# A hybrid decoder layer on one core: modulation products in groups, small inputs turned later, recurrent work spread over the parts of a step

## The chip, the cores and the metric

The kernel runs on one core of a Trainium2 chip. The metric is the device time of one execution in microseconds (us). Three runs of the kernel before gave 2319.43 to 2323.03 us, with a median of 2319.6 us.

## What is computed

One inference step of a decoder layer runs over 256 prompt columns and 8 sample columns (264 in all), with model width 2048, all in 32-bit floats:

```
mod = silu(c) @ w_ada + b_ada                     # 9 vectors sh1 sc1 g1 ... g3 of 2048, for 9 conditions
h = modulate(rmsnorm(x, g_ffn1), sh1, sc1)
x = x + 0.5 * g1 * swiglu(h, w_up1, w_down1)      # inner width 5632
h = modulate(rmsnorm(x, g_mix), sh2, sc2)
x = x + g2 * hybrid_mixer(h)                      # RG-LRU (1024 channels) and SSD (16 heads), one w_out
h = modulate(rmsnorm(x, g_ffn2), sh3, sc3)
x = x + 0.5 * g3 * swiglu(h, w_up2, w_down2)
y = modulate(rmsnorm(x, g_final), shf, scf)       # shf, scf: silu(c) @ w_ada_f, two more vectors
```

In the mixer, the RG-LRU channels pass through a causal convolution of width 4, two gates (small block-diagonal products) and a linear recurrence over time. The SSD channels pass through a convolution and a chunked scan with states. The new states are outputs too.

## The kernel before, in words

All weights stream from device memory once, 533.62 MB in the profiled execution. A weight W is split into a high part (w_hi, a rounded copy made by ScalarE, L608) and a rest (w_lo, a subtraction by VectorE, L878). TensorE makes three products of each 128 x 128 tile: w_hi with the high and with the low part of the activations, and w_lo with the high part (L1379 to L1381).

The work is a written-out list, `plan`, of **steps**. A step has four **parts** (j = 0 to 3) and each part two **pieces** of weights. The kinds of step:

- "up": 1 MB per part, 48 products of 264 columns in a part. 11 steps make a chunk; each of the two FFNs has two chunks.
- "down": three parts of 36 products and one of 24; 8 steps a chunk.
- "xbc", "dt", "lru" (4 steps), "z" (2 steps), "out" (4 steps): the mixer, in this order.

SyncE issues the loads of weights into `raw` (four buffers, one for each part) in the order of the list. The load for part j of a step waits until VectorE has split that part's pieces of the step before (`lo_done`). ScalarE and VectorE split four pieces ahead of TensorE, since w_hi and w_lo have four buffers each. All engines work their instructions off in program order.

The **modulation vectors** are made along the way. A vector takes 16 products (`ada_product`, L1343, eight instructions each, in four column tiles of the array) of 1 MB of w_ada. Vectors 0 and 1 (SH1, SC1) are made before the first step. The nine others ride on the up steps (seven vectors, four steps each) and the first four down steps of the first FFN's two chunks (two vectors): one product stands at the head of each part of such a step. Its 1 MB is loaded just behind the part's weights and waits until all but the last product before it have been made. After the fourth step ScalarE copies the sums out of PSUM (`ada_copy`, L621), TensorE turns them (`ada_turn`, L1323) and VectorE adds the bias (`mod_place`, L900). The first product of the next vector waits for that (`mod_ready`), because it uses the same PSUM bank. Where a segment of the list has two vectors, its four steps are a hardware loop of two turns (except in the first segment, which is written out).

At the start TensorE also turns the prompt and about 20 small inputs into columns (`rows_batch`): the batch for the conditions first, then one behind each of the products 2 to 11 of SH1, the small inputs last. Before those it waits for all small loads (`other_rows`, L1396), which ScalarE issues. VectorE copies each batch out (`place`), then forms the sums of squares, and then runs `mod_place(SH1)`.

In each "lru" step t, ScalarE takes two tiles of channels out of PSUM at part 1 (`conv_first`), VectorE runs the rest of the convolution of both tiles at part 1 (`conv_taps`, L1007 to L1015), and TensorE makes the gates of tile 0 after part 2 and of tile 1 after part 3 (`gates`, L1515), each after a wait for both tiles. At part 0 of the next step ScalarE makes the GELU of the gate branch and a square root (L786, L788). At part 1 of the next step, after `conv_taps`, VectorE runs the recurrence (L1165 to L1177).

Of the kernel before, what the change touches and what calls it, by code (L numbers as in the profile page):

```python
# [21 lines left out]
F32 = mybir.dt.float32  # L22
F32R = mybir.dt.float32r
# [4 lines left out]
P = 128  # L28
D = 2048
# [119 lines left out]
def build(nc, ins, outs):  # L149
    with ExitStack() as ctx:  # L150
# [16 lines left out]
        gate = sb("gate", [P, KD, 9])  # L167
# [21 lines left out]
        def layout(entries):  # L189
# [12 lines left out]
        ada, ada_sum, act_hi, act_lo = layout([  # L202
            ("ada", [P, 2, D], F32), ("ada_sum", [P, 512], F32),
            ("act_hi", [P, KC, COLS], F32R), ("act_lo", [P, KC, COLS], F32R)])

        _, _, ada_more, rowbuf, xrows = layout([
            ("ada_s", [P, 2, D], F32), ("ada_sum_s", [P, 512], F32), ("ada_more", [P, 2, D], F32),
            ("rowbuf", [P, ROW_TILES, P], F32), ("xrows", [P, 2, D], F32)])
        _, _, yrows, ysrow = layout([
            ("ada_e", [P, 2, D], F32), ("ada_sum_e", [P, 512], F32),  # L210
            ("yrows", [P, 2, D], F32), ("ysrow", [P, P], F32)])
# [37 lines left out]
        ada_landed = [sem(f"ada_landed{j}") for j in range(2)]  # L249
        first_landed = [sem(f"first_landed{j}") for j in range(4)]  # L250
# [65 lines left out]
        def ffn_plan(f, s, e, o, vec, up_vecs, down_vecs):  # L316
            for c in range(NCHUNK):
# [138 lines left out]
        def _(sp):  # L456

            def ada_load(a, vec, k):

                if not isinstance(a, int) or a >= 2:  # L460
                    sp.wait_ge(ada_used, a - 1)
# [6 lines left out]
                sp.dma_start(ada[:, k % 2, :], src).then_inc(ada_landed[k % 2], 16)  # L468

            row_copies(sp, True, c_rows)  # L470
            for a in range(2 * KD):
                if a >= 4:
                    sp.wait_ge(ada_used, a - 3)
                dst = (ada, ada_more)[(a // 2) % 2][:, a % 2, :]
                sp.dma_start(dst, w_ada[:, a % KD, bass.ds(a // KD * D, D)]).then_inc(first_landed[a % 4], 16)
# [34 lines left out]
        def _(pool):  # L510
# [8 lines left out]
            pool.memset(outcol[:, OUT_ROWS:], 0.0)  # L519
# [3 lines left out]
            pool.wait_ge(piece_used, 8 * S_XBC)  # L523
            pool.memset(spt[:, :], 0.0)  # L524
# [73 lines left out]
        def _(act):  # L598
# [113 lines left out]
            def act_tasks(kind, t, j):  # L712
# [52 lines left out]
                if kind == "lru":  # L765
# [4 lines left out]
                    if j == 3:  # L770
# [6 lines left out]
                        for h in range(2):  # L777
                            by = lam2[:, 0, 2 * t + h:2 * t + h + 1]
                            act.wait_ge(decay_ready, 2 * t + h + 1)
                            A(th[:, 0, h, :], th[:, 0, h, :], ACT.Tanh, bias=by, scale=by).then_inc(decay_tanh, 1)  # L780
                if (kind == "lru" and j == 0 and t) or (kind == "z" and u == 0):
# [5 lines left out]
                    act.wait_ge(decay_tanh, 2 * (q + 1))  # L787
                    A(th[:, 0, :, :], th[:, 0, :, :], ACT.Sqrt, scale=0.25).then_inc(sqrt_ready, 1)  # L788
# [41 lines left out]
            for n, seg in enumerate(plan):  # L830
                kind, s_first, count, per, vec0, _, _, what = seg
                nxt = last_kind(n)
                for i, last in turns(act, seg, peel_first=n == 0, peel_last=differs(n)):
                    for k in range(per):
                        s, e_, o_, par = at_step(seg, i, k)
                        follows = nxt if last and k == per - 1 else PIECE_KIND[kind]
                        for j in range(4):
                            pieces_ahead(s, j, PIECE_KIND[kind], follows)
                            if kind == "up" and j == 1:
                                act.wait_ge(piece_used, s * 8 + 4)  # L840
                                act.wait_ge(drained[1], o_)
                                A(silu_g[:, :, :], main[:, 0:2, 0:COLS], ACT.Silu).then_inc(drained[0], 1)  # L842
                            if kind not in ("up", "down"):
                                act_tasks(kind, what or 0, j)
                    if vec0 is not None:
                        ada_copy(i + vec0)
# [23 lines left out]
        def _(dve):  # L870
# [37 lines left out]
            def make_gate(vec, factor):  # L908
                dve.wait_ge(mod_ready, vec + 1)
                ch.link(TS(gate[:, :, :], mods[:, vec, :, :], factor, None, ALU.mult))  # L910
# [742 lines left out]
```

## Time and profile before

| | |
|---|---|
| median of three runs | 2319.6 us |
| the profiled execution: its own time | 2320.57 us |
| its span, first to last instruction | 2318.8 us |
| TensorE busy | 2176.4 us (94%) |
| VectorE busy | 1174.0 us (51%) |
| ScalarE busy | 843.5 us (36%) |
| GpSimd busy | 128.0 us (6%) |
| mean granted clock of TensorE | 0.968 of 2.4 GHz |
| moved by DMA | 533.62 MB, a mean of 230 GB/s |

In a timeline row the columns are: start in us, duration in us, engine, line and operation, output<-inputs, tile size, number of instructions merged, and in brackets the idle time before the row with what ended it. Durations of matmuls overlap, since they are pipelined, so the distance from start to start is what one costs. In a row of the waits the columns are: who waited, for whom, us in total, times, longest. A row of the windows gives for each engine the busy us and the count of instructions, then the granted clock, the busy share of the DMA engines and GB/s. "issue" as what ended an idle time means that the profile shows nothing the engine waited for.

### The profile page before, as it was taken

To read this page: it belongs to the slowest core of one execution; us is meant where nothing else is said; L and a number is where in the kernel's file an instruction comes from. 1 tells how busy PE (TensorE), PEld (TensorE's weight loads), DVE (VectorE), ACT (ScalarE), POOL (GpSimd) and SP (SyncE) were. 2 spreads that over 40 slices of the span, in tenths; PEclk is the share of its full clock that TensorE was granted. 3 is DMA by queue.
4 is the path that set the end of the run, shared out by engine and by line. 5 is a ranking of instruction groups with operands and counts; after the bars stand their busy time and mean duration, and the time that the engine had idled before them with its cause. 6 is when DMAs were issued, how large, how long until landed. Compare 5 with 4: busy or idle time off the path is not lost.

```text
span 2318.8 us, 41073 instructions
## 1 busy us (share of the span) xinstructions
PE 2176.4 (94%) x17101; PEld 1972.8 (85%) x17101; DVE 1174.0 (51%) x1583; ACT 843.5 (36%) x1028; POOL 128.0 (6%) x146
## 2 busy tenths in 40 slices
PE   4589999999999999989988989999999999999997
PEld 1178889889878898889987989889999988789996
DVE  1254344345433444566778876535454543344555
ACT  0143233334323333345554543433333333233333
POOL 0000000000000000001467100000000000000000
PEclk8799999999999999999998999999999999999998
DMA  8978895786878867756544555795545689795452
GB/s 345 372 248 297 279 305 192 251 301 217 303 259 290 291 204 265 265 164 184 174 149 146 158 155 178 258 310 177 181 145 177 211 284 301 257 309 181 150 185 87
DMA packets 380730, 533.62 MB, mean 230 GB/s; under 512 B 11815, under 2 KB 356783, under 8 KB 357807
## 3 DMA queue, kind: packets, MB, share of 16 engines
q1 hardware_dynamic: 358288, 519.28, 66.8%
q10 hardware_dynamic: 22303, 12.33, 1.8%
q8 instruction: 107, 1.75, 0.3%
q14 instruction: 32, 0.26, 0.0%
HBM read 524.37 MB, written 7.19 MB: 229 GB/s over the span
## 4 chain that ended last, share of the span: by engine, by line
PE 86%; DVE 7%; DMA 3%; ACT 2%; issue 1%; ACTq 1%; DVEq 0%; SPq 0%
PE main L1379 27%; PE main L1380 25%; PE main L1381 25%; PE b L1343 7%; DVE w_lo L878 2%; DMA ada_more<-in_w_ada 1%; DMA heads_row<-in_ssd_D 1%; ACT w_hi L608 0%; ACTq L445 0%; PE b L1323 0%; DVE cfull L1007 0%; DMA rowbuf<-in_b_ada 0%; DMA raw<-in_w_in 0%; DVE ntile L934 0%; DVE part L983 0%
## 5 line engine op out<-in xcount | busy, mean ns | idle before, releaser
L878 DVE TENSOR_TENSOR w_lo<-raw,w_hi 128x1024 fp32r<-128x1024 f32 (+2 forms) x720 | 797.0, 1114 | 961.6 <-ACT w_hi L608 955.6
L1379 PE MATMUL main<-h_hi,w_hi 128*128 128x264 f32 x3664 | 1069.6, 292 | 33.6 <-DVE w_lo L878 16.3
L608 ACT ACTIVATE w_hi<-raw 128x1024 fp32r<-128x1024 f32 (+2 forms) x720 | 684.0, 956 | 1119.0 <-PE main L1381 1040.9
L1380 PE MATMUL main<-h_lo,w_hi 128*128 128x264 f32 x3664 | 1052.1, 287 | 0.0
L1381 PE MATMUL main<-h_hi,w_lo 128*128 128x264 f32 x3664 | 1050.0, 287 | 0.0
L1379 PEld LDWEIGHTS main<-h_hi,w_hi 128*128 128x128 f32 x3664 | 701.6, 191 | 132.4 <-issue 111.6
L1380 PEld LDWEIGHTS main<-h_lo,w_hi 128*128 128x128 f32 x3664 | 701.1, 191 | 0.5
L1381 PEld LDWEIGHTS main<-h_hi,w_lo 128*128 128x128 f32 x3664 | 699.5, 191 | 0.0
L1379 PE MATMUL main<-act_hi,w_hi 128*128 128x264 f32 x1408 | 403.9, 287 | 0.0
L1381 PE MATMUL main<-act_hi,w_lo 128*128 128x264 f32 x1408 | 400.2, 284 | 0.0
L1380 PE MATMUL main<-act_lo,w_hi 128*128 128x264 f32 x1408 | 399.8, 284 | 0.0
L1379 PEld LDWEIGHTS main<-act_hi,w_hi 128*128 128x128 f32 x1408 | 264.7, 188 | 26.8 <-issue 18.4
L1380 PEld LDWEIGHTS main<-act_lo,w_hi 128*128 128x128 f32 x1408 | 265.4, 189 | 0.0
L1381 PEld LDWEIGHTS main<-act_hi,w_lo 128*128 128x128 f32 x1408 | 264.7, 188 | 0.0
L1343 PE MATMUL b<-ada,cT 128*32 128x512 f32 x1280 | 180.1, 628 | 33.3 <-DMA ada<-in_w_ada 12.1
L1343 PEld LDWEIGHTS b<-ada,cT 128*32 128x32 f32 x1280 | 26.1, 109 | 69.6 <-issue 25.9
L842 ACT ACTIVATE silu_g<-main 128x528 f32<-128x528 f32 x44 | 26.9, 612 | 82.5 <-PE main L1381 82.5
L524 POOL MEMSET spt<- 128x56 f32 x1 | 0.1, 144 | 1024.7 <-PE main L1381 1024.7
L1272 DVE TENSOR_TENSOR part<-silu_g,main 128x528 f32<-128x528 f32 x44 | 31.0, 704 | 32.3 <-PE main L1381 32.3
L951 DVE SCALAR_TENSOR_TENSOR x<-main,gate,x 128x256 f32<-128x256 f32 (+1 forms) x80 | 34.8, 477 | 14.2 <-PE main L1381 14.2
L621 ACT ACTIVATE ada_sum<-b 128x512 f32<-128x512 f32 x11 | 6.4, 583 | 95.0 <-PE b L1343 95.0
L1343 PE MATMUL b<-ada_more,cT 128*32 128x512 f32 x128 | 22.8, 800 | 15.0 <-DMA ada_more<-in_w_ada 15.0
(218 smaller groups left out, 765.1 us busy)
## 6 DMA issues: line engine op xcount, KB each, us to landing
raw<-in_w_up SPq DMA_DIRECT2D x176, 1024.0 KB, 7.4
ada<-in_w_ada SPq DMA_DIRECT2D x128, 1024.0 KB, 5.0
raw<-in_w_down SPq DMA_DIRECT2D x96, 768.0 KB, 4.6
raw<-in_w_in SPq DMA_DIRECT2D x36, 1024.0 KB, 5.3
ada<-in_w_ada_f SPq DMA_DIRECT2D x32, 1024.0 KB, 5.2
ada_more<-in_w_ada SPq DMA_DIRECT2D x16, 1024.0 KB, 9.1
raw<-in_w_down SPq DMA_DIRECT2D x32, 512.0 KB, 3.5
raw<-in_w_out SPq DMA_DIRECT2D x16, 1024.0 KB, 5.2
```

The costliest lines, as they stand in the source:

```text
L524: pool.memset(spt[:, :], 0.0)
L608: A(split_view(w_hi, m, kind), raw_piece(m, kind), ACT.Copy).then_inc(hi_done, 1)
L621: A(ada_sum[:, :], b4[:, :], ACT.Copy).then_inc(ada_copied, 1)
L842: A(silu_g[:, :, :], main[:, 0:2, 0:COLS], ACT.Silu).then_inc(drained[0], 1)
L878: TT(split_view(w_lo, m, kind), raw_piece(m, kind), split_view(w_hi, m, kind).bitcast(F32), ALU.subtract).then_inc(lo_done, 1)
L951: STT(xt, ps[:, h:h + 1, 0:NT], gate[:, bass.ds(n0 + h, 1), 0:1].rearrange("p a b -> p (a b)"), xt, ALU.mult, ALU.add)
L1272: TT(part[:, :, :], silu_g[:, :, :], main[:, 2:4, 0:COLS], ALU.mult).then_inc(drained[1], 1)
L1343: last = MM(b4[32 * j:32 * j + 32, :], cT[:, k, :], src[:, k % 2, j * 512:(j + 1) * 512], start=k == 0, stop=k == KD - 1, tile_position=(0 ...
L1379: MM(out, wh, hi[:, k, :], start=k == 0, stop=False)
L1380: MM(out, wh, lo[:, k, :], start=False, stop=False)
L1381: last = MM(out, wl, hi[:, k, :], start=False, stop=k == total - 1)
```

## The change

1. **Groups.** All the products of a vector for one step stand at the head of the step: four in an up step, two in a down step. The vector of a down chunk now rides on all 8 steps. `ada` has four buffers of 1 MB from the start (`ada_more` goes). Their loads are issued as one burst behind the weights of part 2 of the step before, and a load waits only for the use of its own buffer. `ada_copy`, `ada_turn` and `mod_place` move into parts 1, 2 and 3 of the vector's last step. The gates are scaled in place in `mods`; the tile `gate` and its copy for the mixer's branch go.
2. **Small inputs.** Their two batches and the spread of the heads' constants move behind products 4, 5 and 6 of SC1; VectorE runs `mod_place(SH1)` between the prompt's batches and them.
3. **Recurrent work.** The convolution of tile 0 stays at part 1 and that of tile 1 moves to part 2; gates wait for their own tile. The recurrence up to its states moves to part 0, the product with the GELU stays at part 1. The square root moves to part 3 of the step before, behind the tanh.

```diff
-        ada, ada_sum, act_hi, act_lo = layout([
-            ("ada", [P, 2, D], F32), ("ada_sum", [P, 512], F32),
...
+        ada, act_hi, act_lo = layout([
+            ("ada", [P, 4, D], F32), ("act_hi", [P, KC, COLS], F32R), ("act_lo", [P, KC, COLS], F32R)])
+        ada_sum = outcol[:, 0:512]
...
-                done = 4 * down_vecs[c]
+                done = DNS * down_vecs[c]
                 if done:
-                    plan.append(("down", s, 1, 4, vec, e, o, (f, c, 0)))
-                plan.append(("down", s + done, (DNS - done) // 2, 2, None,
-                             e + done // 2, o + done // 2, (f, c, done)))
+                    plan.append(("down", s, 1, DNS, vec, e, o, (f, c, 0)))
+                else:
+                    plan.append(("down", s, DNS // 2, 2, None, e, o, (f, c, 0)))
...
-                if not isinstance(a, int) or a >= 2:
-                    sp.wait_ge(ada_used, a - 1)
+                if not isinstance(a, int) or a >= 4:
+                    sp.wait_ge(ada_used, a - 3)
...
-                            if vec0 is not None:
+                            if vec0 is not None and j == 2:
                                 vec = i + vec0
-                                if j == 0 and k == 0 and what[0] == 1 and what[2] == 0:
+                                if k == 0 and what[0] == 1 and what[2] == 0:
                                     sp.wait_ge(h_ready, 3 * KD)
-                                ada_load(vec * KD + 4 * k + j, vec, 4 * k + j)
+                                    sp.wait_ge(stored, 16 * (len(OUT_COPIES) + 1))
+                                for q in range(k * KD // per, (k + 1) * KD // per):
+                                    ada_load(vec * KD + q, vec, q)
...
+                        act.wait_ge(decay_tanh, 2 * (t + 1))
+                        A(th[:, 0, :, :], th[:, 0, :, :], ACT.Sqrt, scale=0.25).then_inc(sqrt_ready, 1)
...
                     A(gel[:, :, :], main[:, 2:4, 0:COLS], ACT.Gelu_apprx_tanh).then_inc(drained[1], 1)
-                    act.wait_ge(decay_tanh, 2 * (q + 1))
-                    A(th[:, 0, :, :], th[:, 0, :, :], ACT.Sqrt, scale=0.25).then_inc(sqrt_ready, 1)
...
+                            if vec0 is not None and k == per - 1 and j == 1:
+                                ada_copy(i + vec0)
...
+            def conv_half(idx, j):
+
+                if j == 0:
+                    conv_free(idx)
+                marks = [None, None]
+                for w in (1, 2):
+                    conv_tile(idx, j, marks, w)
+                conv_last(idx, j, marks)
...
-                if kind == "lru" and j == 1:
-                    conv_taps(6 + t)
+                if kind == "lru" and j in (1, 2):
+                    conv_half(6 + t, j - 1)
                 if (kind == "lru" and t) or kind == "z":
                     q = t - 1 if kind == "lru" else 3
-                    if j == 1 and (kind == "lru" or t == 0):
+                    if j == 0 and (kind == "lru" or t == 0):
...
+                    if j == 1 and (kind == "lru" or t == 0):
                         dve.wait_ge(hl_ready, q + 1)
...
                             pieces_ahead(s, j, PIECE_KIND[kind], follows)
+                            if vec0 is not None and k == per - 1 and j == 3:
+                                mod_place(i + vec0)
...
-                ada_product(SH1, k, first=True)
-                if 2 <= k < 2 + batches - 1:
+                ada_product(SH1, k)
+                if 2 <= k < 2 + KD // 2:
                     rows_batch(k - 1)
...
             for k in range(KD):
-                ada_product(SC1, k, first=True)
+                ada_product(SC1, k)
+                if 4 <= k < 4 + N_ROWB:
+                    rows_batch(1 + KD // 2 + k - 4)
...
-                pe.wait_ge(conv_ready, 12 + 2 * (t // 2) + 2)
+                pe.wait_ge(conv_ready, 12 + t + 1)
...
-                            if vec0 is not None:
-                                ada_product(i + vec0, 4 * k + j)
+                            if vec0 is not None and j == 0:
+                                for q in range(k * KD // per, (k + 1) * KD // per):
+                                    ada_product(i + vec0, q)
...
+                            if vec0 is not None and k == per - 1 and j == 2:
+                                ada_turn(i + vec0)
```

`conv_tile` holds one middle tap of one tile and `conv_last` its last tap, both as they stood in `conv_taps`.

## Rows read from the trace of the kernel before

**Rows 1.** The page: busy time by engine, share of the span, instructions.
```profile
PE 2176.4 (94%) x17101; PEld 1972.8 (85%) x17101; DVE 1174.0 (51%) x1583; ACT 843.5 (36%) x1028; POOL 128.0 (6%) x146
```

**Rows 2.** Waits of TensorE: two of its nineteen groups.
```profile
PE b L1515 <- issue: 15.9, 4, 5.3
...
PE b L1343 <- DVE mods L900: 10.6, 2, 8.5
```

**Rows 3.** Timeline of TensorE: products back to back, in parts, and around plain steps.
```profile
54.91 1.07 PE L1343 MATMUL b<-ada,cT 128*32 128x512 f32 x8
55.79 1.04 PE L1343 MATMUL b<-ada_more,cT 128*32 128x512 f32 x8
...
159.82 1.07 PE L1343 MATMUL b<-ada,cT 128*32 128x512 f32 x8
...
166.83 1.06 PE L1343 MATMUL b<-ada,cT 128*32 128x512 f32 x8
...
354.25 0.60 PE L1323 MATMUL b<-ident,ada_sum 128*128 128x128 f32 x4
...
425.35 0.64 PE L1343 MATMUL b<-ada,cT 128*32 128x512 f32 x4
```

**Rows 4.** Timeline of TensorE: the start, and the first step of the second FFN.
```profile
49.70 1.08 PE L1323 MATMUL b<-ident,rowbuf 128*128 128x128 f32 x4 [8.38 <-DMA heads_row<-in_ssd_D]
...
84.36 1.94 PE L1343 MATMUL b<-ada_more,cT 128*32 128x512 f32 x8 [0.56 <-DMA ada_more<-in_w_ada]
...
104.30 1.94 PE L1343 MATMUL b<-ada_more,cT 128*32 128x512 f32 x8 [1.47 <-DMA ada_more<-in_w_ada]
...
117.58 0.59 PE L1379 MATMUL main<-h_hi,w_hi 128*128 128x264 f32 x1 [6.72 <-DVE w_lo L878]
...
138.78 1.07 PE L1343 MATMUL b<-ada,cT 128*32 128x512 f32 x8
...
1453.48 0.56 PE L1379 MATMUL main<-h_hi,w_hi 128*128 128x264 f32 x1 [4.64 <-DVE h_lo L929]
```

**Rows 5.** Timeline where one vector follows another, and branches by line.
```profile
235.31 1.23 DVE L878 TENSOR_TENSOR w_lo<-raw,w_hi 128x1024 fp32r<-128x1024 f32 x1 [2.88 <-ACT w_hi L608]
...
236.87 0.60 PE L1323 MATMUL b<-ident,ada_sum 128*128 128x128 f32 x4
...
239.55 1.02 PE L1343 MATMUL b<-ada,cT 128*32 128x512 f32 x5 [2.08 <-DVE mods L900]
...
248.15 0.64 PE L1343 MATMUL b<-ada,cT 128*32 128x512 f32 x4
...
690.20 1.05 PE L1343 MATMUL b<-ada,cT 128*32 128x512 f32 x5 [3.61 <-issue]
...
L367 PEldq COMPARE_BRANCH  x32: 76/208/4987, 376.1 to 2291.9; - x32
```

**Rows 6.** The recurrent steps: windows of two steps, and timelines of three engines.
```profile
1196.70:1238.10 41.40, 33.54 (x251) 31.12 (x250) 32.71 (x44) 20.69 (x32) 27.24 (x23) 0.92 0.50 153
1238.10:1278.00 39.90, 34.29 (x256) 33.10 (x256) 34.49 (x42) 20.85 (x30) 28.43 (x24) 0.91 0.55 166
...
1185.44 1.22 PE L1515 MATMUL b<-cval,gates_w 128*128 128x264 f32 x2 [5.00 <-issue]
...
1178.86 2.83 DVE L1007 SCALAR_TENSOR_TENSOR cfull<-cin,small,cfull 128x288 f32<-128x288 f32 x4 [0.91 <-ACT cfull L670]
...
1184.11 1.23 DVE L1015 SCALAR_TENSOR_TENSOR cval<-cin,small,cfull 128x8 f32<-128x8 f32 x1
...
1169.62 1.28 ACT L788 ACT_TABLE_LOAD   x1
```

**Rows 7.** SyncE's queue and TensorE around the last down step of a chunk; loads on the page.
```profile
564.35 0.37 SPq L489 DMA_DIRECT2D raw<-in_w_up  x1
...
573.87 0.64 PE L1343 MATMUL b<-ada,cT 128*32 128x512 f32 x4
...
ada<-in_w_ada SPq DMA_DIRECT2D x128, 1024.0 KB, 5.0
```

More of the change, by code:

```diff
@@ L248, in build @@
         w_landed = [sem(f"w_landed{j}") for j in range(4)]
-        ada_landed = [sem(f"ada_landed{j}") for j in range(2)]
-        first_landed = [sem(f"first_landed{j}") for j in range(4)]
+        ada_landed = [sem(f"ada_landed{j}") for j in range(4)]
         hi_done, lo_done = sem("hi_done"), sem("lo_done")
@@ L909, in make_gate @@
                 dve.wait_ge(mod_ready, vec + 1)
-                ch.link(TS(gate[:, :, :], mods[:, vec, :, :], factor, None, ALU.mult))
+                ch.link(TS(mods[:, vec, :, :], mods[:, vec, :, :], factor, None, ALU.mult))
             def norm_samples():
@@ L943, in norm, with add_branch @@
                 lo(KD - 1)
-            def add_branch(s, par, before, n0, squares):
+            def add_branch(vec, s, par, before, n0, squares):
                 dve.wait_ge(piece_used, s)
@@ L974, in place @@
                     dve.tensor_copy(x[:, k:k + 2, 0:NT], bank[:, :].rearrange("p (k n) -> p k n", k=2)).then_inc(rows_placed, 1)
-            for b in range(1 + N_ROWB + KD // 2):
+            for b in range(1 + KD // 2):
+                place(b)
+            mod_place(SH1)
+            for b in range(1 + KD // 2, 1 + N_ROWB + KD // 2):
                 place(b)
@@ L987, in _ @@
                     TT(sumsq[:, :, :], sumsq[:, :, :], part2[:, :, :], ALU.add).then_inc(sumsq_ready, 1)
-            mod_place(SH1)
             mod_place(SC1)
@@ L1000, in conv_taps, with conv_tile, conv_last @@
                     dve.wait_ge(gate_made, 2 * (idx - 6))
+            def conv_tile(idx, j, marks, w):
+                tap, _ = conv_params(idx, j)
+                dve.wait_ge(conv0_ready, 2 * idx + j + 1)
+                if w == 2:
+                    ch.wait(marks[j])
+                marks[j] = ch.add(STT(cfull[:, j, :], cin[:, idx % 2, j, w:w + COUT], tap(w),
+                                      cfull[:, j, :], ALU.mult, ALU.add))
+            def conv_last(idx, j, marks):
+                tap, _ = conv_params(idx, j)
+                ch.wait(marks[j])
+                STT(cval[:, j, 0:NT], cin[:, idx % 2, j, 3:3 + NT], tap(3), cfull[:, j, 0:NT], ALU.mult, ALU.add)
+                win = cfull[:, j, SAMP0 - 0:SAMP0 + 4 * NB - 3:4]
+                STT(cval[:, j, NT:COLS], windows(idx % 2)[:, j, :, 3], tap(3), win,
+                    ALU.mult, ALU.add).then_inc(conv_ready, 1)
@@ L1009, in conv_taps @@
-                        marks = [mark] if j == 0 and w == 1 else marks + [mark]
-                ch.wait()
-                for j in range(2):
-                    tap, _ = conv_params(idx, j)
-                    STT(cval[:, j, 0:NT], cin[:, r, j, 3:3 + NT], tap(3), cfull[:, j, 0:NT], ALU.mult, ALU.add)
-                    win = cfull[:, j, SAMP0 - 0:SAMP0 + 4 * NB - 3:4]
-                    STT(cval[:, j, NT:COLS], windows(r)[:, j, :, 3], tap(3), win,
-                        ALU.mult, ALU.add).then_inc(conv_ready, 1)
+                        conv_tile(idx, j, marks, w)
@@ L1280, in _ @@
                                 n0 = i * (2 * per) + 2 * (what[2] + k)
-                                add_branch(s * 8 + 8, par, (e_, o_)[par], n0, squares)
+                                add_branch((G1, G3)[what[0]], s * 8 + 8, par, (e_, o_)[par], n0, squares)
                             if kind not in ("up", "down"):
                                 dve_tasks(kind, what or 0, j, s, o_, e_)
-                    if vec0 is not None:
-                        mod_place(i + vec0)
                 if kind == "down" and squares and (n + 1 == len(plan) or plan[n + 1][0] != "down"):
@@ L1327, in turn_part, with ada_product @@
                 return MM(out, src, ident[0:rows, 0:rows], start=True, stop=True)
-            def ada_product(vec, k, first=False):
-                if first:
-                    src = (ada, ada_more)[(k // 2) % 2]
-                    pe.wait_ge(first_landed[k % 4], 16 * (vec * 4 + k // 4 + 1))
-                else:
-                    src = ada
-                    pe.wait_ge(ada_landed[k % 2], (vec - 2) * (8 * 16) + 16 * (k // 2 + 1))
+            def ada_product(vec, k):
+                pe.wait_ge(ada_landed[k % 4], vec * (4 * 16) + 16 * (k // 4 + 1))
                 if k == 0:
```

54 lines of the change are left out of this document (20 added, 34 removed).

## The prediction

> **What bounds the kernel now.** I read the page first. TensorE is busy 94% of the span, and the other engines half of it or less [rows 1], so a gain is either TensorE work that gets cheaper or a gap of TensorE that closes. The waits of TensorE, read next, show which gaps lie near the change: four waits of the gates (15.9 us, put down to "issue", though a row below shows whom they wait for) and two waits of products for `mods` (10.6 us, of which 8.5 at the start) [rows 2]. Then I went through TensorE's timeline stage by stage. In the steps that carry a vector TensorE has no gap at all: a product costs it array time and nothing else. At the start it waits for loads. In the recurrent steps it waits for VectorE. The change touches all three.
>
> **1. Products in groups.** Three plain up steps run from the turn at 354.25 to the product at 425.35: 71.1 us less about 0.5 for the turn is 23.5 us a step, 5.88 a part. A part with a product takes 166.83 - 159.82 = 7.01 us, so a product between pieces costs 1.13 us. Two products back to back start 55.79 - 54.91 = 0.88 us apart [rows 3]. Each product that joins another saves therefore 0.25 us, and a little more for those inside a run; I take 0.26. Bounds: 0, if the one back-to-back pair is a lucky case, and 0.30.
> Of 28 up steps with a vector, the first of each FFN belongs to other terms. The other 26 merge three times: 26 x 3 x 0.26 = 20.3 us. The two down vectors have 32 products in 16 groups: 16 x 0.26 = 4.2 us. Spreading them over 8 steps instead of 4 changes nothing else for TensorE. Together 24.5 us (0 to 28).
> In the second FFN's first step TensorE is idle 4.64 us before its first piece, waiting for the norm [rows 4]. All four products now stand in or ahead of that gap, three more than before: 3 x 1.13 = 3.4 us (2 to 6; at the top the clock, which stands at half after this gap, does not fall).
>
> **2. Where one vector follows another.** Before, the sums are turned at 236.87, and the next product starts at 239.55 after 2.08 us of waiting for `mod_place`; the next part begins at 248.15 [rows 5]. That is 11.3 us for a turn (0.4) and a part (7.01), so 3.9 us are lost, a part of it to the half clock that follows the wait. After the change the turn stands at part 2 and `mod_place` in VectorE's part 3, just behind a split that ended at 235.31 + 1.23 = 236.54 [rows 5]. With about 0.5 us of its own it ends some 0.2 us after TensorE gets there. I leave 0.4 and take 3.5 us (2 to 4).
> The other two places (turn at 686 and 1973) are back edges of hardware loops. There the product came after 3.61 us of "issue", and the branch in TensorE's queue takes up to 4.99 us against a median of 0.21 [rows 5]. The change keeps these loops with bodies as long as before, so the branch stays. I take 0.7 us each, 1.4 in all (0 to 16: the top is both stalls hidden).
>
> **3. The start.** TensorE sits idle for 8.38 us before 49.70, until the last small load has landed, with eleven products made; `mods` cost 8.5 more [rows 2, 4]. With at most four loads outstanding the loads run dry in both. Undisturbed they come (104.30 - 84.36) / 8 = 2.49 us apart [rows 4]. From 41.3 us, 21 products at that pace need 52.3, and the last ends near 95 instead of 106.2. The small loads now have until product 20 (near 65 us) and share the DMA engines longer, which I charge 1 us.
> Not all of these 11 us arrive. The first step now wants four products at its head, and their loads come behind 3 MB of weights: 7 MB at 2.49 us or somewhat more land at about 112, so the first piece starts near 113 instead of 117.58. Its eight pieces need 23.5 us and, by my estimate, 1.5 for the norm, which feeds the first four pieces only as it goes. The second step starts near 138. Before, it started at 138.78 + 7.01 = 145.8 [rows 4]. Gain 8 us (5 to 11).
>
> **4. Recurrent steps.** The four middle taps of both tiles run from 1178.86, the last taps end at 1184.11 + 1.23 = 1185.34, and the gates start at 1185.44 after 5.00 us: this "issue" wait is for VectorE's convolution [rows 6]. One tile is half of it, about 3.3 us instead of 6.5. The first gates start some 3 us earlier, the second tile runs while TensorE works on the next pieces, and the recurrence moves into a gap that VectorE has in part 0. With less idle time the half clock of this stretch goes in part.
> What limits the gain is VectorE: it is busy 32.71 of 41.40 us in one step and 34.49 of 39.90 in the next [rows 6], so a step cannot lose more than about 7 us. I take 4 us for three steps, 12 in all. Bounds: 4 (1.3 a step, if the moved square root delays the splits as much as the halves hasten the gates) and 20.
> The square root costs a table load of 1.28 us [rows 6]. Before, it stood beside the GELU's load. Now one more set of functions comes between exponentials, so up to one load is added per step, and the first splits of the next step stand 1.9 us later (load and root) with about 1 us of slack: that is in the 4 us. The Trainium skill ("ScalarE: Activation LUTs", section "Table sets: the hidden batching unit") prices a change of set at about 2.7 us, and says that tanh and square root are in different sets. By that the delay grows by 1.4 us in three steps and the forecast by up to 4; the trace has 1.28 for it, and the sum goes by the trace.
>
> **5. What the burst costs.** Before, each 1 MB of `w_ada` came behind 1 MB of weights. Now four stand behind the weights of part 2, and the weights of part 3 behind them. In a steady step those weights are let go when piece 5 is split, about 12.5 us into a step of 27. A load alone lands in 5.0 us [rows 7] and each further one 2.49 later, so the fourth product's lands at about 12.5 + 5.0 + 4 x 2.49 = 27.5 us and is used at 27.2 + 2.6 = 29.8. That holds by some 2 us.
> It does not hold where an up step with a vector follows a down step, which is shorter. There the weights go at 564.35 and the products start at 573.87 [rows 7]. The fourth load lands near 564.7 + 5.0 + 10 = 579.7, its product wants it at 576.5. This happens twice: I charge 3 us each, 6 in all (0 to 12).
> The gates scaled in place and the copy that goes are VectorE work of a fraction of a microsecond behind TensorE's pieces: nothing.
>
> **Sum.** 24.5 + 3.4 + 3.5 + 1.4 + 8 + 12 = 52.8, less 6 and 0.4 for small waits: 46.4 us. The profiled execution's own time is 2320.57, its span 2318.8, so 2274; the median of the runs is 1 us lower. Two of my terms (the merge inside a run and the late burst) are on the careful side, and I say **2272 us**.
>
> **The rivals.**
> *The burst comes late in every step* (slower). Margin 2 us. If VectorE splits piece 5 later than I think, or the loads run slower in a burst, each of 26 steps waits for its fourth product. A wait of 2.08 us was followed by a part of 8.60 instead of 7.01 us [rows 5], so a wait of 1 us may cost 2.6 with the half clock: 26 x 2.6 = 68, 2340 us. It decides from 1.8 us a step on, that is, from loads some 3 us later than computed. Against it: the same bytes flow now without a gap. 5%.
> *VectorE binds the recurrent steps*: the wait moves from the gates to the splits, and only some 3 of the 12 us are left: 2281. For it: GpSimd is busy 27 us of each such step [rows 6], and does the same work in a shorter step. The Trainium skill ("SBUF — State Buffer", section "SBUF: two separate sides") says that the port these two engines share is an exclusive lock, held for a whole instruction. By that VectorE's busy time would not shrink with the step, and its 33 to 34 us are the floor; I counted with it. 15%.
> *A product in a group costs what it costs alone*: 24.5 us go, 2296. Against it stands the pair in [rows 3]. 6%.
> *The loops' back edges are hidden too*, since the turn no longer stands before the branch: 13 us more, 2259. Against it: the branch reaches only some 2 us ahead of the array, and takes 5. 9%.
> *The parts eat each other up* and nothing measurable is left: 2%.
>
> **How the numbers follow.** The forecast has 63%; its terms, each to its bounds but not all at once, spread it over some 2258 to 2286. The range reaches to the VectorE and the back-edge rival and leaves out the slower one and half of the one on groups: 2252 to 2290. A difference of 0.2% is about what a measurement of this kernel can tell from no change. Faster 93%, same 2%, slower 5%.
>
> **What would show it.** Steady up steps with a vector 27.2 to 27.3 us apart, the four products within 3.5 us and without a gap; 2.0 us for two in a down step; no wait of 8 us before 60 us, and the last product of SC1 near 95; a gap under 1 us between the second and third vector, but 5-us branches still there in the two loops; gates of tile 0 waiting under 2 us, recurrent steps of 36 to 38 us; a wait of some 3 us for loads at the first products after each down chunk. Wrong would make it above all a wait for w_ada at every group, or a clock at half in the steps with products.

## The result, and the profile after

The changed kernel takes **2268.5 us** (median of four runs, 2266.8 to 2269.1) against 2320.0 us of the kernel before, measured beside it. The ratio is 0.9779, with a 95% interval from 0.9764 to 0.9793. Its profiled execution has a span of 2266.4 us, 52.4 less than before. The forecast was 2272 us, in a range of 2252 to 2290.

The head of the page shows what kind of gain it is. TensorE's busy time fell by 33.6 us [rows 1] and its share rose to 95%; so part of the gain is cheaper products, and the rest are gaps.

```profile
PE 2142.8 (95%) x17101; PEld 1968.3 (87%) x17101; DVE 1173.7 (52%) x1582; ACT 848.9 (37%) x1031; POOL 126.5 (6%) x146
```

The waits of TensorE over the whole span (who, for whom, total, times, longest) answer to [rows 2]:

```profile
PE b L1356 <- DMA ada<-in_w_ada: 45.4, 42, 7.2
PE b L1356 <- issue: 9.1, 2, 4.6
...
PE b L1529 <- DVE cval L1013: 5.6, 2, 2.8
...
PE b L1356 <- DMA ada<-in_w_ada_f: 2.9, 2, 1.5
PE b L1529 <- issue: 2.4, 2, 1.7
```

L1356 is the product (L1343 before) and L1529 the gates (L1515 before). The four waits of the gates went from 15.9 us to 8.0 (5.6 + 2.4). Most of the 45.4 us for w_ada lies at the start; from 143 us on there are 6.6 of them, and 2.9 for the last two vectors' loads, where the kernel before had none. The two waits put down to "issue" are the back edges of the two loops.

TensorE's timeline, place by place:

```profile
138.76 2.78 PE L1356 MATMUL b<-ada,cT 128*32 128x512 f32 x24
141.87 1.06 PE L1356 MATMUL b<-ada,cT 128*32 128x512 f32 x8 [0.33 <-DMA ada<-in_w_ada]
...
166.53 3.64 PE L1356 MATMUL b<-ada,cT 128*32 128x512 f32 x32
...
193.76 3.64 PE L1356 MATMUL b<-ada,cT 128*32 128x512 f32 x32
...
549.86 1.92 PE L1356 MATMUL b<-ada,cT 128*32 128x512 f32 x16 [1.50 <-DVE mods L895]
552.34 1.06 PE L1356 MATMUL b<-ada,cT 128*32 128x512 f32 x8 [0.55 <-DMA ada<-in_w_ada]
554.91 1.06 PE L1356 MATMUL b<-ada,cT 128*32 128x512 f32 x8 [1.50 <-DMA ada<-in_w_ada]
...
666.33 5.15 PE L1356 MATMUL b<-ada,cT 128*32 128x512 f32 x32 [4.57 <-issue]
...
1402.69 3.64 PE L1356 MATMUL b<-ada,cT 128*32 128x512 f32 x32
...
1433.74 1.92 PE L1356 MATMUL b<-ada,cT 128*32 128x512 f32 x16
1436.72 1.06 PE L1356 MATMUL b<-ada,cT 128*32 128x512 f32 x8 [1.06 <-DMA ada<-in_w_ada]
...
1929.94 6.51 PE L1356 MATMUL b<-ada,cT 128*32 128x512 f32 x32 [4.56 <-issue]
```

The steady step is 193.76 - 166.53 = 27.23 us long, against 4 x 7.01 = 28.04 before [rows 3], with its four products in one run of 3.64 us. The second step starts at 138.76. At 549.86, behind the first down chunk, the group takes 6.11 us instead of 3.64, because its last two products wait for their loads. At 666.33, behind a loop's back edge, it takes 5.15 without any wait for a load: the granted clock of that stretch is 0.70, that is, partly at 1.2 GHz, after 4.57 us of idling. At 1929.94, behind the other loop's back edge, it takes 6.51 at 0.55.

The gain of each stage, from start to start in the two timelines, beside the terms of the prediction:

| term | predicted | measured |
|---|---|---|
| products in groups, 26 up steps | 20.3 | 21 (26 x 0.81) |
| the same, two down vectors | 4.2 | 2.5, with 3.1 lost in groups that late loads made longer |
| first step of the second FFN | 3.4 | 4.3 |
| second vector to third | 3.5 | 3.6 |
| two back edges | 1.4 | 3.3 (2.8 and 0.5) |
| start | 8 | 14.0 |
| recurrent steps | 12 | 8.2 |
| late bursts in up steps, by the length of the groups | -6 | -8.9 (2.5, 2.9, 3.5) |
| other waits | -0.4 | -1.5 (for `mods`, at 549.86) |
| not foreseen: xbc stage, output stage | 0 | 5.1 (3.0 and 2.1) |
| sum | 46.4 | 51.6 of 52.4 |

### The profile page after: what moved, and what is told of

The parts are those of the page before. It is cut to its first block, busy times and chain, and to the rows that moved or that the text cites. A ratio compares the mean times of both kernels' runs of the same rounds, so it can differ in the third digit from the quotient of the medians.

```text
span 2266.4 us, 40943 instructions
## 1 busy us (share of the span) xinstructions
PE 2142.8 (95%) x17101; PEld 1968.3 (87%) x17101; DVE 1173.7 (52%) x1582; ACT 848.9 (37%) x1031; POOL 126.5 (6%) x146
## 4 chain that ended last, share of the span: by engine, by line
PE 80%; DMA 8%; DVE 7%; ACT 2%; issue 1%; POOL 1%; SPq 1%; ACTq 0%; DVEq 0%; POOLq 0%
PE main L1392 25%; PE main L1393 24%; PE main L1394 24%; DMA ada<-in_w_ada 7%; PE b L1356 6%; DVE w_lo L873 2%; ACT w_hi L603 1%; DMA ada<-in_w_ada_f 1%; DVE ntile L929 1%; DVE h_lo L924 0%; SPq L464 0%; PE b L1341 0%; DVE rec L1187 0%; POOL state L566 0%; DVE rstd L917 0%
## 5 line engine op out<-in xcount | busy, mean ns | idle before, releaser
L1392 PE MATMUL main<-h_hi,w_hi 128*128 128x264 f32 x3664 | 1056.2, 288 | 19.3 <-DVE h_lo L924 7.9
L1356 PE MATMUL b<-ada,cT 128*32 128x512 f32 x1408 | 189.7, 658 | 59.7 <-DMA ada<-in_w_ada 45.4
L1356 PEld LDWEIGHTS b<-ada,cT 128*32 128x32 f32 x1408 | 38.4, 114 | 164.9 <-DMA ada<-in_w_ada 92.4
L946 DVE SCALAR_TENSOR_TENSOR x<-main,mods,x 128x256 f32<-128x256 f32 (+1 forms) x80 | 34.8, 476 | 12.9 <-PE main L1394 12.9
L616 ACT ACTIVATE outcol<-b 128x512 f32<-128x512 f32 x11 | 6.5, 592 | 83.0 <-PE b L1356 83.0
L1297 DVE TENSOR_TENSOR act_lo<-part,act_hi 128x528 f32 (+1 forms) x44 | 31.2, 708 | 4.0
```

The lines of the kernel that those rows point to most:

```text
L616: A(ada_sum[:, :], b4[:, :], ACT.Copy).then_inc(ada_copied, 1)
L946: STT(xt, ps[:, h:h + 1, 0:NT], mods[:, vec, bass.ds(n0 + h, 1), 0:1].rearrange("p a b -> p (a b)"), xt, ALU.mult, ALU.add)
L1297: TT(act_lo[:, bass.ds(pair * 2, 2), :], part[:, :, :], hi.bitcast(F32), ALU.subtract).then_inc(act_ready, 1)
L1356: last = MM(b4[32 * j:32 * j + 32, :], cT[:, k, :], ada[:, k % 4, j * 512:(j + 1) * 512], start=k == 0, stop=k == KD - 1, tile_position=(0 ...
L1392: MM(out, wh, hi[:, k, :], start=k == 0, stop=False)
```

## The experiments

Each run is an edit of the changed kernel (2268.5 us, span 2266.4), and was timed against the kernel before. A time is the median of its runs; "span" is how much longer the span of its one profiled execution is than 2266.4 us.

**Products taken apart.** One product per part again, loads, copy, turn and bias as they stood before.

```diff
-                            if vec0 is not None and j == 0:
-                                for q in range(k * KD // per, (k + 1) * KD // per):
-                                    ada_product(i + vec0, q)
+                            if vec0 is not None and (per == 4 or j % 2 == 0):
+                                ada_product(i + vec0, 4 * k + j if per == 4 else 2 * k + j // 2)
...
```

> The changed kernel (2268.5 us) with its products taken apart again: one product at the head of each part of an up step, one at parts 0 and 2 of a down step, each load behind that part's weights, the sums copied and turned behind the last step; four buffers, the small inputs and the recurrent steps stay as changed. Theory (a product in a group is 0.27 us cheaper, and the boundary between vectors is hidden): a steady up step goes back from 27.22 to 28.05 us, the boundary between the second and third vector gets its 2 us wait back, the late bursts (some 13 us of waits for loads) go; in sum 25 us slower, 2290 to 2297. Rival (most of the gain came from the loads and buffers, a product costs the same alone): steps stay near 27.3 us and the time rises by 3 to 8 us, 2272 to 2276.

2294.0 us, ratio 0.9888 (0.9868 to 0.9909), span +24.4. The step is back at four parts of 7.02 us, and so is the wait at the boundary:

```profile
204.57 1.07 PE L1356 MATMUL b<-ada,cT 128*32 128x512 f32 x8
211.59 1.06 PE L1356 MATMUL b<-ada,cT 128*32 128x512 f32 x8
...
228.20 1.06 PE L1356 MATMUL b<-ada,cT 128*32 128x512 f32 x8 [2.08 <-DVE mods L895]
```

The theory holds: groups and boundaries, less the late bursts that came with them, are nearly half of the gain of 51.5 us.

**Small inputs back in the first vector.** The batches and the heads' constants go back behind products 10 to 12 of SH1.

```diff
-            for b in range(1 + KD // 2):
-                place(b)
-            mod_place(SH1)
-            for b in range(1 + KD // 2, 1 + N_ROWB + KD // 2):
+            for b in range(1 + N_ROWB + KD // 2):
                 place(b)
...
+            mod_place(SH1)
             mod_place(SC1)
...
```

> The changed kernel with the batches of small inputs and of the heads' constants back behind the products 10 to 12 of the first vector, and its bias added only after the sums of squares. Theory (the whole gain of the start is the move of the small inputs): the wait of some 8 us before 60 us comes back, the last product of SC1 ends near 106 us instead of 94.2, and the time is 10 to 14 us longer, 2278 to 2283. Rival (the start gains because four buffers and four products at the head of the first step let the loads run on): the last product of SC1 moves, but the first step's end stays within 3 us of 138.8, 2269 to 2272.

2283.7 us, ratio 0.9838 (0.9822 to 0.9854), span +15.2, just over the top of the theory. Both stops are back (L1339 is the turn, L1354 the product in this kernel):

```profile
50.04 1.08 PE L1339 MATMUL b<-ident,rowbuf 128*128 128x128 f32 x4 [10.42 <-DMA heads_row<-in_ssd_D]
...
68.68 3.64 PE L1354 MATMUL b<-ada,cT 128*32 128x512 f32 x16 [8.31 <-DVE mods L895]
```

The second step starts at 149.3 instead of 138.8.

**The recurrent part, in pieces.** Three things changed there: the halves (the convolution of the two tiles at two parts), the early recurrence and the early root. Four runs take back all of it, the root alone, the root and the early recurrence (so that only the halves stay), and the halves alone.

```diff
-                        act.wait_ge(decay_tanh, 2 * (t + 1))
-                        A(th[:, 0, :, :], th[:, 0, :, :], ACT.Sqrt, scale=0.25).then_inc(sqrt_ready, 1)
...
                     A(gel[:, :, :], main[:, 2:4, 0:COLS], ACT.Gelu_apprx_tanh).then_inc(drained[1], 1)
+                    act.wait_ge(decay_tanh, 2 * (q + 1))
+                    A(th[:, 0, :, :], th[:, 0, :, :], ACT.Sqrt, scale=0.25).then_inc(sqrt_ready, 1)
...
-                    if j == 0 and (kind == "lru" or t == 0):
+                    if j == 1 and (kind == "lru" or t == 0):
...
-                if kind == "lru" and j in (1, 2):
-                    conv_half(6 + t, j - 1)
+                if kind == "lru" and j == 1:
+                    conv_taps(6 + t)
...
-                pe.wait_ge(conv_ready, 12 + t + 1)
+                pe.wait_ge(conv_ready, 12 + 2 * (t // 2) + 2)
```

The first edit is the root, the second the recurrence, the last two are the halves. All taken back:

> The changed kernel with its recurrent steps as before: the convolution of both tiles at part 1, the gates wait for both, the recurrence behind it at part 1, the square root behind the GELU. Theory (the spread itself gained 8 us in the four steps, by gates that wait less): the steps go back to 28.0, 39.0, 41.4 and 40.2 us, 2276 to 2278. Rival (VectorE is the limit and the steps gained by something else, such as the clock they start with): within 3 us of 2268.5.

The root alone taken back:

> The changed kernel with only the square root back at part 0 behind the GELU; the two halves of the convolution and the recurrence at part 0 stay. Theory (as predicted, the moved root costs a table load of 1.28 us per step in front of the next step's splits): 1 to 4 us faster than 2268.5. Rival (the recurrence at part 0 now waits for GELU, load and root, and the convolution behind it on VectorE comes late): 2 to 8 us slower, 2271 to 2277, with the longer wait at the gates of tile 0.

Root and recurrence taken back:

> The changed kernel with the recurrence back at part 1 behind the convolution and the square root back behind the GELU; only the split of the convolution into two halves, and the gates that wait for their own tile, stay. Theory (the halves are what gains, the rest is balance): the recurrent stage stays within 2 us of its 216.4 us between the totals at 1083.2 and 1299.5, 2267 to 2271. Rival (the recurrence at part 1 delays VectorE's second half as much as the split hastens the first): stage near the 224.5 us of the kernel with everything undone, 2275 to 2279.

The halves alone taken back:

> The changed kernel with the convolution of both tiles back at part 1 in one piece, the gates waiting for both; the recurrence at part 0 and the square root at part 3 stay. Measured so far for the recurrent stage, between the totals: everything undone 224.5 us, halves alone 225.4, halves and the early recurrence 222.2, all three 216.4. Theory A (the early recurrence with the early root is what gains, the halves add little): stage 217 to 219, time 2269 to 2271. Theory B (the halves are needed, since both tiles at part 1 make the first gates wait some 3 us longer in each step, and only the early recurrence gives VectorE the room for them): stage 221 to 225, time 2273 to 2277.

The stage is taken on TensorE, from a small product in the last xbc step to the total ahead of the output steps. In the changed kernel these are the two rows

```profile
1083.15 0.69 PE L1548 MATMUL b<-sumsq,ones 8*128 8x256 f32 x2
...
1299.51 0.68 PE L1369 MATMUL b<-sumsq,ones 128*128 128x264 f32 x2 [2.08 <-DVE sumsq L1235]
```

and the same two in every other run. The kernel before took 224.6 us for it.

| halves | early recurrence | early root | stage, us | time, us | ratio to before (95%) |
|---|---|---|---|---|---|
| yes | yes | yes | 216.4 | 2268.5 | 0.9779 (0.9764 to 0.9793) |
| no | no | no | 224.5 | 2280.1 | 0.9824 (0.9808 to 0.9840) |
| yes | yes | no | 222.2 | 2274.3 | 0.9796 (0.9780 to 0.9812) |
| yes | no | no | 225.4 | 2279.7 | 0.9834 (0.9818 to 0.9850) |
| no | yes | yes | 215.1 | 2269.1 | 0.9771 (0.9754 to 0.9789) |

The halves bring nothing, alone or beside the others (the 1.3 us that the stage is shorter without them is not seen in the times). The early root, which I had priced as a cost, is worth 5.8 us beside the early recurrence. TensorE's waits between 1080 and 1262 us show why the halves bring nothing, first of the changed kernel and then of the one without halves:

```profile
PE b L1529 <- DVE cval L1013: 5.6, 2, 2.8
PE main L1392 <- DVE w_lo L873: 2.7, 3, 1.3
PE b L1529 <- issue: 2.4, 2, 1.7
PE b L1460 <- DVE xdec L1053: 2.1, 1, 2.1
PE b L1483 <- DVE s L1172: 1.8, 1, 1.8
```

```profile
PE b L1529 <- issue: 14.9, 4, 5.3
PE main L1392 <- DVE w_lo L873: 0.6, 1, 0.6
```

With halves the gates wait 8.0 us, without them 14.9; but the whole is 14.6 against 15.5 us. The wait has only moved from the gates to the splits, the states and the state block, and each of these is a wait for VectorE, which is busy 32.0 us in a step of 37.2 (third figure of this row of the windows):

```profile
1146.80:1184.00 37.20, 33.02 (x248) 30.95 (x249) 32.02 (x45) 21.91 (x32) 27.12 (x25) 0.95 0.55 170
```

The root shows in VectorE's own waits between 1095 and 1262 us. With the root behind the GELU, and then in the changed kernel:

```profile
DVE th L1182 <- ACT th L783: 11.3, 4, 3.5
DVE w_lo L873 <- ACT w_hi L603: 8.4, 5, 3.1
```

```profile
DVE w_lo L873 <- ACT w_hi L603: 15.1, 6, 3.9
```

With the root behind the GELU, VectorE stands some 3 us at the recurrence four times, for ScalarE's GELU and root, and everything behind it is late. In the changed kernel that wait is gone. VectorE waits longer for the splits instead, but the two together fall from 19.7 to 15.1 us, and all of TensorE's waits between 1080 and 1262 us from 20.1 to 14.6 us, nearly the 5.8 us of the stage. So the early recurrence and the early root together are the gain: beside the halves, the recurrence alone takes the stage from 225.4 to 222.2 us, and the root takes it to 216.4. The early root without the early recurrence was not run, so what it is worth alone is not shown.

**The burst one part earlier.**

```diff
-                            if vec0 is not None and j == 2:
+                            if vec0 is not None and j == 1:
                                 vec = i + vec0
```

> The changed kernel with the burst of w_ada issued behind the weights of part 1 instead of part 2, one part (about 6 us) earlier. Theory (the waits for loads at the first groups after a down chunk, after the loops' back edges and in the down steps, some 13 us in all, are lateness of the burst): 8 to 13 us faster, 2255 to 2261, and the group at 549.9 us takes about 3.6 us instead of 7.6. Rival (the loads are limited by bandwidth there, or the weights of part 2 come late behind the burst): steady steps longer than 27.23 us, no gain or slower, 2267 to 2280.

2250.7 us, ratio 0.9699 (0.9678 to 0.9719), span -17.8: more than the theory's 13. SyncE's queue, in the changed kernel and here (start, time from the first to the last issue, number):

```profile
528.95 9.73 SPq L482 DMA_DIRECT2D raw<-in_w_up  x3
538.97 2.19 SPq L464 DMA_DIRECT2D ada<-in_w_ada  x4
...
1390.89 32.44 SPq L482 DMA_DIRECT2D raw<-in_w_up  x4
1423.37 2.18 SPq L464 DMA_DIRECT2D ada<-in_w_ada  x4
```

```profile
528.25 3.89 SPq L482 DMA_DIRECT2D raw<-in_w_up  x2
532.43 2.97 SPq L464 DMA_DIRECT2D ada<-in_w_ada  x4
...
1395.48 4.11 SPq L464 DMA_DIRECT2D ada<-in_w_ada  x4
```

Behind the down chunk the burst starts 6.5 us earlier. For the second step of the second FFN it starts at 1395.48 instead of 1423.37, which was 10.4 us ahead of its group at 1433.74. From 143 us on no group waits for a load any more (timeline of TensorE):

```profile
549.17 3.64 PE L1356 MATMUL b<-ada,cT 128*32 128x512 f32 x32 [1.50 <-DVE mods L895]
...
662.04 3.64 PE L1356 MATMUL b<-ada,cT 128*32 128x512 f32 x32 [3.38 <-issue]
...
1424.92 3.64 PE L1356 MATMUL b<-ada,cT 128*32 128x512 f32 x32
...
1913.01 5.34 PE L1356 MATMUL b<-ada,cT 128*32 128x512 f32 x32 [3.02 <-issue]
```

Of the 17.8 us, 8.9 are the three late groups in up steps and 3.1 those in down steps. Another 5.4 are the two back edges (at 662.04 and 1913.01, gap and group together 2.7 us less at each), which became shorter although nothing was changed there.

**The two loops written out on TensorE.**

```diff
-                for i, last in turns(pe, seg, peel_first=n == 0):
+                for i, last in turns(pe, seg, peel_first=n == 0 or vec0 is not None):
```

> The changed kernel with the two hardware loops of two vectors written out on TensorE alone; the other engines keep theirs. Theory (the 4.6 us waits at 661.8 and 1929.9 us are the branch and the fetch behind it, and the slow group after each is the clock at half that follows): 9 to 13 us faster, 2256 to 2260. Rival 1 (the wait is for the bias that VectorE adds behind its own loop's branch): a wait of 2 to 4 us stays under another name, 2264 to 2267. Rival 2 (the group there is late because of its loads): the wait stays in whole, within 1 us of 2268.5.

2257.3 us, ratio 0.9730 (0.9709 to 0.9751), span -14.1; by the medians it is 11.2 us, since the profiled execution was the fastest of the four. Branches of TensorE's queue (count; shortest, median and longest in ns), in the changed kernel, with the early burst, and here:

```profile
L363 PEldq COMPARE_BRANCH  x28: 76/208/6535, 352.2 to 2239.4; - x28
```

```profile
L363 PEldq COMPARE_BRANCH  x28: 76/208/5295, 352.6 to 2221.3; - x28
```

```profile
L363 PEldq COMPARE_BRANCH  x24: 76/210/243, 351.8 to 2224.4; - x24
...
661.09 3.64 PE L1356 MATMUL b<-ada,cT 128*32 128x512 f32 x32
...
1917.73 3.64 PE L1356 MATMUL b<-ada,cT 128*32 128x512 f32 x32
```

Without the branch there is no gap at either place and no slow group behind it: 4.57 + 5.15 - 3.64 = 6.1 us at the first, 4.56 + 6.51 - 3.64 = 7.4 at the second. Neither VectorE's bias nor the loads were waiting to take its place.

**The second convolution ahead of the state block** in part 2 of the last recurrent step.

```diff
+                if kind == "lru" and u == 14:
+                    conv_half(9, 1)
...
-                if kind == "lru" and j in (1, 2):
+                if kind == "lru" and j in (1, 2) and u != 14:
```

> The changed kernel with VectorE's convolution of the second tile ahead of the state block in part 2 of the last recurrent step. Theory (that step is 1.0 us longer than before because the second convolution stands behind the state block): the wait of 1.7 us before its last gates goes, step 39.5 instead of 41.2 us, 1 to 2 us faster, 2266.5 to 2267.5. Rival (the state block is then late and TensorE's states wait for it as long): within 0.5 us of 2268.5.

2272.5 us, ratio 0.9793 (0.9775 to 0.9811), span +0.9, by the medians +4.0: no gain, and not told apart from a small loss. The waits of TensorE in that step say why. The state block now ends later, and what needs its banks waits 5.0 us, against 1.8 + 1.7 for the state block and the last gates in the changed kernel:

```profile
PE b L1485 <- DVE s L1174: 5.0, 1, 5.0
```

**Early burst and written-out loops together.**

> The burst behind the weights of part 1 and the two loops of two vectors written out on TensorE, both together. Alone they took 17.8 and 14.1 us off the span of 2266.4 us. Theory (they share only the two back edges, where the earlier burst already took 2.7 us each off the gap and the slow group behind it): 17.8 + 14.1 - 5.4 = 26.5 us faster, span 2240, time 2242. Rival (with the loops gone the groups meet their loads late again): groups at the two places longer than 4 us, 2246 or more.

2240.7 us, ratio 0.9668 (0.9654 to 0.9682), span 2237.0, that is -29.4 (27.8 by the medians), somewhat more than the sum says. Every group in a steady step takes 3.64 us. It has the lowest median of all the versions here.

**The same, with the first step's four products apart.**

```diff
...
-                            if vec0 is not None and j == 0:
+                            if n == 0 and i == 0 and k == 0:
+                                ada_product(vec0, j)
+                            elif vec0 is not None and j == 0:
```

> The same, and the four products of the first step alone stand one at the head of each part again, each load behind that part's weights. Theory (the group at the head of the first step holds back the norm's pieces until the loads of all four products have landed, which cost 4.3 us in the kernel with all products apart: second step at 134.4 instead of 138.8 us): 4 to 5 us faster than the run with both, some 2238. Rival (the pieces of the first step then wait for the norm and the second step's burst is late): within 1.5 us of it.

2244.0 us, ratio 0.9679 (0.9665 to 0.9693), span +5.1 against the run with both: not faster. The times alone hardly tell the two apart, but the traces show a loss. The second step starts, in the run with both and here, at

```profile
136.61 3.64 PE L1356 MATMUL b<-ada,cT 128*32 128x512 f32 x32
```

```profile
141.07 3.64 PE L1358 MATMUL b<-ada,cT 128*32 128x512 f32 x32
```

The expectation rested on a misread timeline. In the run with all products apart 134.44 is the product of part 3, and the second step starts one part later, at 141.5, later than the changed kernel's 138.8. The timeline of this run shows that the first step's pieces wait for VectorE's splits even with no group ahead of them:

```profile
105.85 0.59 PE L1394 MATMUL main<-h_hi,w_hi 128*128 128x264 f32 x1 [6.77 <-DVE w_lo L875]
...
122.41 0.39 PE L1394 MATMUL main<-h_hi,w_hi 128*128 128x264 f32 x1 [2.35 <-DVE w_lo L875]
```

The group uses time in which many of them could not run anyway.

## Why the prediction was right, and where it was not

The forecast of 2272 us missed the time by 3.5, and that is in part luck. The table's terms came out 6.0 (start), 5.1 (not foreseen) and 1.9 us (back edges) better than predicted, and 3.8 (recurrent steps), 2.9 (late bursts), 1.7 (down vectors) and 1.1 us (other waits) worse. The groups in up steps and the boundary, which are nearly half of the gain, were right in themselves.

1. **Groups: right, in mechanism and size.** 0.26 us for each product that joins another gave 20.3 us; the steps show 21, and taking the groups apart gives them back.
2. **Boundaries: right.** 3.5 predicted, 3.6 found; TensorE has no wait there any more. In the two loops the branch stayed, as predicted, and writing out the loops, which left no gap, shows that it is the cause. The term of 1.4 us was too small by 2, with 2.8 us at the first edge and 0.5 at the second; why they differ was not tried.
3. **Start: the end was right, the beginning misread.** The second step starts at 138.76, predicted 138. But the row at 138.78 [rows 4] is the product of part 2, not of part 3. The second step of the kernel before started at 138.78 + 2 x 7.01 = 152.8, not 145.8. The part left out of the count hid 7 us of gain; the last expectation above repeats the slip. The move of the small inputs carries most of the 14.0 us: its undoing costs 10.5 of them up to the second step, and 1.6 more by the third, in a group that waits longer for its loads.
4. **Recurrent steps: the size was off, and the reason wrong.** I counted 12 us, 4 in each of three steps, from gates that start 3 us earlier. From the gates of tile 1 to the next ones these steps take 35.5, 37.2 and 40.4 us, before 39.0, 41.3 and 39.9: the last gains nothing. The gates do wait 7 us less, and this is worth nothing, as the rival on VectorE said: the wait moves to the splits and the states. The gain of 8.2 us is that of the early recurrence with the early root. The step that failed is the price of the root, "up to one load is added per step" as a loss: the root left the part in which VectorE's recurrence stood behind it (TensorE's waits for `w_lo` fell from 6.0 to 2.7 us, those for ScalarE's `spread_b` from 3.5 us to none). The Trainium skill's page "ScalarE: Activation LUTs" (section "Table sets: the hidden batching unit") advises against another change of set, and its 2.7 us would have made the cost higher still. The runs went the other way: between 1080 and 1310 us the changed kernel makes 19 table loads, the one with the root behind the GELU 16, and the stage with the three more loads (3 x 1.28 us of ScalarE) is 5.8 us shorter. Where a load stands weighed more than how many there are. The last step was not mended by the other order of its two VectorE jobs.
5. **Late bursts: the mechanism right, one place missed.** Each place costs 2.5 to 3.5 us, predicted 3. There are three in up steps, not two: the second step of the second FFN is the third. There SyncE's four loads of weights ahead of the burst took 32.44 us to be issued, so it came 10.4 us ahead of its group, where a steady step has some 14 (565.13 for the group at 579.57). The down steps, which I took as safe, lose another 3.1 us in all, 2.0 of them as waits. That the margin holds in the other up steps was right; but for 0.5 us in the second step, behind the start, none of their groups is longer for its loads.
6. **Not foreseen: 5.1 us** in the xbc and output stages. In the xbc stage the kernel before waits 3.2 us (at 1072.46) for ScalarE to copy the sums of the dt step out of PSUM (L716), behind a split that had waited 1.80 us for its weights; between 1060 and 1080 us the granted clock is 0.91. In the changed kernel the two waits are 2.0 and 0.64 us, and the clock between 1028 and 1048 us is 1.00. Why that load lands earlier was not tried. In the output stage the trace of the kernel before points to a part of the change, the copy into `gate`. It stands on VectorE ahead of a split that TensorE waits for, and holds it up by 0.4 us:

```profile
1354.02 0.23 DVE L910 TENSOR_SCALAR gate<-mods 128x144 f32<-128x144 f32 x1
...
1356.24 0.39 PE L1379 MATMUL main<-h_hi,w_hi 128*128 128x264 f32 x1 [1.95 <-DVE w_lo L878]
```

In the changed kernel, without the copy, this wait is 1.20 us, and the granted clock in the 7 us behind it is 1.00 in place of 0.76. The prediction had put the copy at nothing, as work behind TensorE's pieces; at this place it stood ahead of one. No run put it back, so how much of the 2.1 us it explains is not shown. All the kernels of the experiments have these some 5 us, but for 1.0 us that the output stage takes longer with the whole recurrent part taken back, and with the second convolution ahead of the state block.

The rows of "what would show it" came out so: 27.23 us per step, 3.64 for four products (I said 3.5) and 1.92 for two, the last product of SC1 ended at 94.1, the branches were still there. The boundary has no gap. The gates of tile 0 wait 2.8 us twice, where I wanted under 2, and of the recurrent steps of 36 to 38 us the last is the miss, with 40.4.

## What to carry to other kernels

Put small matmuls of another tile shape side by side, and then issue their loads as a burst early enough for the shortest step that comes ahead, not the average one: the same change with the burst one part earlier gained 18 us more. A shorter wait is no gain by itself: where the engine that is waited for is busy for most of the step, add up all of TensorE's waits in the stage before and after, as one sum. Before a timeline row is used as the start of a step, count the parts up to it.

## What the runs showed of the hardware that was not expected

- The branch at the end of a large loop body took longer where more loads were in flight. The two of the changed kernel take 6.54 and 6.52 us, with the DMA engines' busy share at 1.07 meanwhile and 357 to 358 GB/s. The six of the kernel before, of the one with the products apart and of the one with the burst behind part 1 take 4.95 to 5.50 us, at 0.51 to 0.57 and 176 to 195 GB/s. The median branch takes 0.21 us. The DMA records show a packet of 16 KB of instructions while such a branch runs: it starts 3.9 us after the branch in the changed kernel, 2.9 and 2.4 us with the earlier burst. That the branch waits for it, and that it comes late because of the loads, fits these times, but no run tested it.
- How long TensorE idled did not alone tell the clock behind the gap. After 4.57 and 4.56 us the granted clock was 0.70 and 0.55 in the group that follows, and 32 matmuls took 5.15 and 6.51 us in place of 3.64. After 3.38 us it stayed at 1.00, but after 3.02 us in the same run it was 0.68, and the group took 5.34. What decided it is not shown.
